# A weight ring's first refills in fewer transfers, on one core of Trainium2

## The chip, the core and the metric

One core of a Trainium2 chip runs the whole kernel. The metric is the device time of one execution in microseconds. The kernel before was run three times: 1255.82, 1257.26 and 1256.54 us, median 1256.54. Times inside a profile are counted from the first instruction of the profiled execution.

## The reference, cut to what matters

One layer of a streaming encoder on 256 tokens of width 1024, float32. A combined projection feeds two token mixers (RWKV-7 and a gated MLP over chunks), their gated sum goes through an output projection, and then comes the part that this case is about, a mixture of 32 experts, of which each token uses four:

```python
def expert_block(args):
    tok, e = args
    hgu = xt[tok] @ w_gate_up[e] + b_gate_up[e]
    gate = jnp.minimum(hgu[:, 0::2], SWIGLU_LIMIT)
    up = jnp.clip(hgu[:, 1::2], -SWIGLU_LIMIT, SWIGLU_LIMIT)
    act = gate * jax.nn.sigmoid(SWIGLU_ALPHA * gate) * (up + 1.0)
    return act @ w_down[e] + b_down[e]
```

`w_gate_up[e]` is 1024 x 2048 and `w_down[e]` 1024 x 1024, both float32: 12 MiB of weights for each expert, 384 MiB in all, and every byte of them is read once.

## The kernel before, in words

**Phases.** Up to about 340 us the kernel does the mixers and the output projection. Then it goes through the 32 experts in order (`moe`). Each expert has 64 slots for its tokens. TensorE gathers the tokens of a pair of experts by matmuls with a one-hot matrix, multiplies them with the expert's gate/up weights (`gate_up`, matmuls on L1602), transposes the activations, multiplies them with the down weights (`down`, L1627) and scatters the result back to the token rows in PSUM (`scatter`, L1656). Down and scatter of an expert run behind the gate/up of the next.

**Pieces and ring.** The weights are cut into 96 pieces (`PIECES`) of 4 MiB, 32 KB in each of 128 partitions: two for an expert's gate/up matrix and one for its down matrix. In each partition a piece is 32 KB in one run, in HBM and in SBUF. Their order is that in which TensorE reads them: 0 and 1 are gate/up of expert 0, 2 and 3 gate/up of expert 1, 4 down of expert 0, 5 and 6 gate/up of expert 2, 7 down of expert 1, 8 and 9 gate/up of expert 3, 10 down of expert 2, and so on. They go through a ring of five buffers (`RING`); piece n lies in buffer n mod 5. So piece 5 refills the buffer of piece 0, piece 7 that of piece 2, piece 12 that of piece 7.

**Who waits for whom.** TensorE counts `pieces_read` up by one for each quarter of a piece that it has multiplied with, four a piece (L1604, L1629). All loads of the ring are issued by SyncE, one after the other, on one queue (`weights`, from L461); before each it waits until TensorE has read that part of the piece that lay there. A load counts its buffer's semaphore `ring_full` up when it has landed. TensorE waits for that semaphore at the start of a piece for all loads of the piece (L1595, L1621), also where the piece came in several; only the last three pieces (`TAIL_PARTS`) have a semaphore for each part. How many loads a piece comes in is set by `fills(n)` (L348): four for piece 5, two for the other pieces below 10, one from piece 10 on. `fill_of` adds them up, so that both sides count alike, and in `weights` the part of the older piece that must have been read is worked out from it as well:

```python
for i in range(fills(n)):
    sp.wait_ge(sm["pieces_read"], quarters_read(*reader, 4 * (i + 1) // fills(n)))
    load_part(n, i, fills(n))
```

**The preload.** The first five pieces are loaded while the mixers still run, since their buffers lie where the mixers' data lay; a list written by hand (L440 to L459) gives the order of the halves and what each has to wait for: 0a, 0b, 2a, 1a, 1b, 3a, 2b, 4b, 3b, 4a (a and b are a piece's halves). The halves of piece 1 stand behind the wait for `y_done`, one behind the other, and that of piece 3 follows without a wait. The last two, 3b and 4a, wait for the output projection. `more_passes` would go through all experts again if one of them had more tokens than slots; with these inputs there is one pass, and the branch is not taken.

Of the kernel before, what the change touches and what calls it, by code (L numbers as in the profile page):

```python
# [67 lines left out]
def build(nc, cst, x, norm1_g, w_in, b_gate, time_mix, w_decay_up, w0, a_up, a0, g_up, k_k, k_a, r_k,  # L68
# [8 lines left out]
    with ctx:  # L77
# [95 lines left out]
        RING = len(SLOT_AT)  # L173
# [135 lines left out]
        unit_of = [("a", n, n % 8) for n in range(NA)] + [("v", n, 4 - 4 * n) for n in range(2)]  # L309
        unit_of += [("f", j, (2 * j + 4) % 8) for j in range(len(f_loads))] + [("o", k, (k + 4) % 8) for k in range(KT)]  # L310
        unit_load = {(kind, n): (u, 1 + sum(v == u for _, _, v in unit_of[:i])) for i, (kind, n, u) in enumerate(unit_of)}

        def unit_sem(kind, n):
# [31 lines left out]
        def slot_of(n):  # L345
            return n % RING

        def fills(n):  # L348

            return 4 if n == RING else 2 if n < 2 * RING else 1  # L350

        def fill_of(p, n):
            return p * sum(fills(m) for m in range(slot_of(n), PIECES, RING)) + sum(fills(m) for m in range(slot_of(n), n + 1, RING))
# [39 lines left out]
        def _(sp):  # L393
# [35 lines left out]
            def load(n, lo, hi, full):  # L429
                sp.dma_start(ring[slot_of(n)][:, lo:hi], pieces[n][:, lo:hi]).then_inc(full, 16)  # L430

            def load_part(n, i, parts=2):
                load(n, i * PIECE // parts, (i + 1) * PIECE // parts, ring_full[slot_of(n)])
# [13 lines left out]
            sp.wait_ge(sm["gl_done"], KT)  # L447
            load_part(2, 0)
            sp.wait_ge(sm["y_done"], NCH)
            load_part(1, 0)  # L450
            load_part(1, 1)
            load_part(3, 0)
            sp.wait_ge(sm["m_ready"], KT * NCH)
            load_part(2, 1)
# [6 lines left out]
            def weights(p, read_count=None):  # L461
                for n in range(RING if read_count is not None else 0, PIECES):
                    if read_count is not None and n == PIECES // 2:
                        read_count()
                    reader = (p, n - RING) if n >= RING else (p - 1, max(range(n, PIECES, RING)))
                    if n < 2 * RING:
# [3 lines that stand above are left out]
                    else:  # L470
                        sp.wait_ge(sm["pieces_read"], quarters_read(*reader))
                        if n in TAIL_PARTS:
                            load_tail(n)
                        else:
                            load(n, 0, PIECE, ring_full[slot_of(n)])
# [1275 lines left out]
```

## Time and profile before

| What | Before |
| --- | --- |
| Median of three runs | 1256.54 us |
| Profiled execution | 1257.94 us |
| Its span, first to last instruction | 1256.1 us |
| Granted TensorE clock, mean | 0.991 |
| TensorE busy | 1198.1 us, 95% of the span |
| VectorE, ScalarE busy | 293.6 us, 188.7 us |
| Moved by DMA | 447.78 MB, mean 356 GB/s |
| The queue with the ring's loads (q1) | 439.93 MB, 85.3% of 16 engines' time |
| Chain of waits that ended last | PE 71%, DMA 27% |

The span is what the profile shows; the execution's own time has 1.8 us around it. The granted clock is the share of TensorE's full clock that it was given. The chain of waits is followed back from the last instruction, at each step to what released it.

In the rows below, times are microseconds from the span's start. SPq is SyncE's queue: its rows are issues of transfers, and "DMA to landing" is the time from an issue to the last byte's arrival, as the semaphore tells it. All ring loads have the line L430. An issue itself takes 0.33 to 0.43 us. Landing time less issue time therefore holds the wait behind older transfers, too. Where two or three issues share a row, the times to landing are the least, the middle and the longest of them. In rows 3, 4 and for piece 9 a later issue has the longer time; for pieces 7 and 8 (two issues each, in the middle the mean) the first issue has the longer one and the second the shorter.

### The profile page before, as it was taken

How to read it: one execution, taken by the hardware profiler on the slowest of the kernel's cores; microseconds unless marked ns; L12 is line 12 of the kernel's file. 1: busy time of each engine (PE TensorE's matmuls, PEld its weight loads, DVE VectorE, ACT ScalarE, POOL GpSimd, SP SyncE). 2: the span in 40 equal slices, each digit the busy share in tenths (PEclk: the TensorE clock that was granted, in tenths of full speed). 3: DMA queues.
4: the chain of work that ended last, by engine and by line, in shares of the span. 5: the costliest groups of instructions: out<-in, count | busy, mean ns of one | idle time of the engine just before them, and what ended most of it. 6: DMA issues, size and time to landing. Idle time of an engine off the chain costs nothing.

```text
span 1256.1 us, 16267 instructions
## 1 busy us (share of the span) xinstructions
PE 1198.1 (95%) x7267; PEld 580.2 (46%) x7267; DVE 293.6 (23%) x639; ACT 188.7 (15%) x359; POOL 11.1 (1%) x24
## 2 busy tenths in 40 slices
PE   5999999999999999999998989999999989899997
PEld 4788668876533433434333333334333333333332
DVE  1155473334412111121111111111212111111111
ACT  2363212323200001000000100010000000000102
POOL 1000000000000000000000000000000000000000
PEclk9999999999999999999999999999999999999999
DMA  8451668347999999999999999999999999999994
GB/s 228 118 141 45 201 187 219 87 156 305 377 407 409 430 426 434 434 430 433 428 431 431 430 431 429 430 434 434 431 427 428 433 431 434 432 431 427 430 425 185
DMA packets 71244, 447.78 MB, mean 356 GB/s; under 512 B 12516, under 2 KB 51550, under 8 KB 56704
## 3 DMA queue, kind: packets, MB, share of 16 engines
q1 hardware_dynamic: 60864, 439.93, 85.3%
q0 software_dynamic: 1456, 4.36, 1.1%
q10 hardware_dynamic: 8848, 2.38, 0.8%
q8 instruction: 60, 0.98, 0.3%
q14 instruction: 16, 0.13, 0.0%
HBM read 444.56 MB, written 2.10 MB: 356 GB/s over the span
## 4 chain that ended last, share of the span: by engine, by line
PE 71%; DMA 27%; DVE 1%; issue 0%; ACT 0%; SPq 0%; DVEq 0%; ACTq 0%
PE ps L1602 27%; DMA ring<-w_gate_up 26%; PE ps L1213 8%; PE ps L1627 8%; PE ps L1301 7%; PE ps L1587 4%; PE ps L1656 3%; PE ps L1489 2%; PE ps L1288 2%; PE ps L1610 2%; PE ps L1646 1%; PE ps L1637 1%; PE ps L1241 1%; DMA consts<-cst 1%; PE ps L1551 1%; PE ps L1260 0%
## 5 line engine op out<-in xcount | busy, mean ns | idle before, releaser
L1602 PE MATMUL ps<-ring,xacc 128*64 128x512 f32 x2048 | 467.1, 603 | 27.0 <-DMA ring<-w_gate_up 25.6
L1602 PEld LDWEIGHTS ps<-ring,xacc 128*64 128x64 f32 x2048 | 144.0, 138 | 316.4 <-issue 310.1
L1627 PE MATMUL ps<-ring,aT 128*64 128x512 f32 x992 | 218.8, 593 | 7.5 <-DMA ring<-w_down 7.5
L1627 PEld LDWEIGHTS ps<-ring,aT 128*64 128x64 f32 x992 | 74.0, 137 | 148.1 <-issue 148.1
L1162 DVE TENSOR_SCALAR gc<-ps 128x512 f32<-128x512 f32 x32 | 22.1, 692 | 394.4 <-PE ps L1602 394.4
L1118 DVE TENSOR_TENSOR xacc<-ps,vec 128x512 f32<-128x512 f32 x32 | 22.1, 692 | 343.2 <-PE ps L1587 343.2
L1213 PE MATMUL ps<-hT,wbuf 128*128 128x256 f32 (+1 forms) x432 | 99.4, 388 | 2.8 <-DVE hT L811 2.8
L1213 PEld LDWEIGHTS ps<-hT,wbuf 128*128 128x128 f32 (+1 forms) x432 | 81.7, 191 | 18.4 <-issue 3.1
L1301 PE MATMUL ps<-hT,wbuf 128*128 128x256 f32 x384 | 85.9, 382 | 0.1
L1301 PEld LDWEIGHTS ps<-hT,wbuf 128*128 128x128 f32 x384 | 72.1, 190 | 11.8 <-issue 2.2
L770 ACT ACTIVATE sgm<-gc 128x512 f32<-128x512 f32 x32 | 20.2, 632 | 372.0 <-DVE gc L1162 372.0
L1587 PEld LDWEIGHTS ps<-oh,x2p 128*128 128x128 f32 x512 | 60.6, 194 | 27.6 <-issue 26.5
L1587 PE MATMUL ps<-oh,x2p 128*128 128x128 f32 x512 | 66.7, 284 | 0.9 <-DVE oh L1081 0.9
L1656 PE MATMUL ps<-ysl,oht 64*128 64x512 f32 x248 | 61.9, 616 | 0.7 <-ACT ysl L749 0.7
L759 ACT ACTIVATE oht<-ps 128x256 f32<-128x256 f32 x32 | 12.3, 384 | 253.7 <-PE ps L1637 253.7
L749 ACT ACTIVATE ysl<-ps 128x512 f32<-128x512 f32 x31 | 18.5, 597 | 177.3 <-PE ps L1627 177.3
L1610 PE MATMUL ps<-biases,consts 32*64 32x512 f32 x256 | 34.8, 612 | 0.0
L1169 DVE TENSOR_TENSOR gc<-uc,sgm 128x512 f32<-128x512 f32 x32 | 34.2, 1069 | 1.8 <-ACT sgm L770 0.8
L1656 PEld LDWEIGHTS ps<-ysl,oht 64*128 64x128 f32 x248 | 21.3, 186 | 21.5 <-issue 20.0
L1489 PE MATMUL ps<-wbuf,XM 128*128 128x512 f32 x64 | 28.5, 595 | 0.3 <-DVE XM L994 0.3
L1288 PE MATMUL ps<-wbuf,hT 128*128 128x512 f32 x64 | 28.0, 592 | 0.0
L1165 DVE SCALAR_TENSOR_TENSOR uc<-uc,gc 128x512 f32<-128x512 f32 x32 | 22.1, 692 | 1.1
(259 smaller groups left out, 677.4 us busy)
## 6 DMA issues: line engine op xcount, KB each, us to landing
ring<-w_gate_up SPq DMA_DIRECT2D x55, 4096.0 KB, 36.0
ring<-w_down SPq DMA_DIRECT2D x28, 4096.0 KB, 34.5
ring<-w_gate_up SPq DMA_DIRECT2D x16, 2048.0 KB, 11.6
wbuf<-w_in SPq DMA_DIRECT2D x26, 512.0 KB, 4.0
wbuf<-w_in SPq DMA_DIRECT2D x12, 1024.0 KB, 6.5
ring<-w_down SPq DMA_DIRECT2D x6, 2048.0 KB, 12.2
wbuf<-w_in SPq DMA_DIRECT2D x2, 2048.0 KB, 9.9
wbuf<-w_out SPq DMA_DIRECT2D x8, 512.0 KB, 4.8
```

Of the source, the lines that this page charges most:

```text
L1118: V.tensor_tensor(by_k(xT[pair % 2])[:, 4 * half:4 * half + 4, :], by_k(bank(b)), vec[:, r:r + 4].unsqueeze(2).to_broadcast([P, 4, 2 * SLO ...
L1162: V.tensor_scalar(gc[:, :], pairs[:, 0, :], LIMIT, None, ALU.min).then_inc(sm["gc_ready"], 1)
L1169: V.tensor_tensor(acts[:, :].rearrange("q (r p) -> q p r", r=4), by_row(uc), by_row(sgm), MUL).then_inc(sm["act_ready"], 1)
L1213: last = mm(proj_slot(n)[0:w, :], wv[:, k, 0:w], hv[:, k, :], start=k == 0, stop=k == KT - 1)
L1288: last = mm(bank(m_), hv[:, k, tb * P:(tb + 1) * P], wv[:, k, :], start=k == 0, stop=k == KT - 1)
L1301: last = mm(f_slot(t), wv[:, k, P * (t % 2):P * (t % 2) + P], hv[:, k, :], start=k == 0, stop=k == KT - 1, skip_group_check=True)
L1489: last = mm(bank(2 * tb + half_), XM_v[:, k, tb * P:(tb + 1) * P], unit((k + 4) % 8)[:, 512 * half_:512 * half_ + 512], start=k == 0, stop ...
L1587: last = mm(bank(b, (k % 4) * 2 * SLOTS, 2 * SLOTS), x2p[:, tb * D + k * P:tb * D + (k + 1) * P], oh[pair % 2][:, tb * 2 * SLOTS:(tb + 1) ...
L1602: last = mm(bank(GU_BANK + q, 0, 512, slice(64 * half, 64 * half + 64)), x_, w[:, :, half, :], start=k == 0, stop=k == KT - 1, skip_group_ ...
L1610: mm(bank(GU_BANK + q, 0, 512, slice(64 * half, 64 * half + 64)), ident[r, 32 * q + e:32 * q + e + 1].to_broadcast([32, SLOTS]), bgu[r, :] ...
L1627: last = mm(bank(b, 0, 512, slice(64 * half, 64 * half + 64)), turned[:, c0:c0 + SLOTS], w[:, D * r + 512 * half:D * r + 512 * (half + 1)] ...
L1656: last = mm(bank(OUT_BANK + 2 * tb + half), oht[e % 2][r, tb * P:(tb + 1) * P], slots[r, :], start=e == 0 and isinstance(p, int), stop=Fal ...
```

## The change

`fills` gives two loads to pieces 0, 2, 3, 4, 5 and 6 and one to all others. Piece 5 (`RING`) is thus refilled in halves and not in quarters, pieces 7, 8 and 9 in one load and not in halves, and piece 6 in halves as it was. In the preload the two halves of piece 1 become one load of the whole piece at the same place. The bytes, the buffers and TensorE's code stay as they are.

```diff
         def fills(n):
 
-            return 4 if n == RING else 2 if n < 2 * RING else 1
+            return 2 if n in (0, 2, 3, 4, RING, RING + 1) else 1
...
             sp.wait_ge(sm["y_done"], NCH)
-            load_part(1, 0)
-            load_part(1, 1)
+            load_part(1, 0, 1)
             load_part(3, 0)
             sp.wait_ge(sm["m_ready"], KT * NCH)
```

## Rows read from the trace of the kernel before

**Rows 1.** Engines' busy time by stretch (us, instructions), granted clock, DMA share, GB/s:

```profile
core 0: us, PE busy (x) PEld busy (x) DVE busy (x) ACT busy (x) POOL busy (x), PEclk, DMA share, GB/s
329.00:333.00 4.00, 3.60 (x17) 2.07 (x16) 1.96 (x6) 0.87 (x2) 0.00 (x0) 1.00 0.28 74
418.00:615.00 197.00, 197.00 (x990) 74.59 (x989) 32.74 (x65) 16.40 (x30) 0.00 (x0) 1.00 1.00 431
615.00:1200.00 585.00, 554.86 (x2702) 210.75 (x2698) 91.31 (x176) 44.59 (x81) 0.00 (x0) 0.99 1.00 431
```

**Rows 2.** TensorE's waits at the ring, 340 to 615 and 615 to 1240; one matmul group:

```profile
  DVE uc L1163: 1.4, 1
...
  DMA ring<-w_gate_up: 25.6, 14
...
1210.38 4.92 PE L1602 MATMUL ps<-ring,xacc 128*64 128x512 f32 x14 [2.64 <-DMA ring<-w_gate_up]
```

**Rows 3.** SyncE's issues from 303.3 to 304.5: 1a, 1b and 3a.

```profile
L430 SPq DMA_DIRECT2D ring<-w_gate_up x3: 327/432/434, 303.4 to 304.2; - x3
...
DMA to landing us min/median/max: 8.7/13.2/17.7
```

**Rows 4.** Issues of 3b and 4a, the preload's last, in this order of landing:

```profile
L430 SPq DMA_DIRECT2D ring<-w_gate_up x1: 328/328/328, 331.5 to 331.5; - x1
L430 SPq DMA_DIRECT2D ring<-w_down x1: 433/433/433, 331.9 to 331.9; - x1
...
DMA to landing us min/median/max: 7.4/10.8/14.2
```

**Rows 5.** Three issues: second quarter of piece 5, its fourth, second half of piece 6.

```profile
L430 SPq DMA_DIRECT2D ring<-w_gate_up x1: 327/327/327, 344.2 to 344.2; - x1
...
DMA to landing us min/median/max: 7.0/7.0/7.0
...
L430 SPq DMA_DIRECT2D ring<-w_gate_up x1: 327/327/327, 348.8 to 348.8; - x1
...
DMA to landing us min/median/max: 7.3/7.3/7.3
...
L430 SPq DMA_DIRECT2D ring<-w_gate_up x1: 328/328/328, 355.6 to 355.6; - x1
...
DMA to landing us min/median/max: 12.4/12.4/12.4
```

**Rows 6.** Issues of pieces 7, 8 and 9, two halves each, from 362.8:

```profile
L430 SPq DMA_DIRECT2D ring<-w_down x2: 328/328/328, 362.8 to 368.2; - x2
...
DMA to landing us min/median/max: 9.6/9.9/10.2
...
L430 SPq DMA_DIRECT2D ring<-w_gate_up x2: 327/328/328, 371.6 to 377.2; - x2
...
DMA to landing us min/median/max: 10.5/10.8/11.1
...
L430 SPq DMA_DIRECT2D ring<-w_gate_up x2: 328/328/328, 380.6 to 384.1; - x2
...
DMA to landing us min/median/max: 11.9/12.6/13.3
```

**Rows 7.** Issues of pieces 10, 11 and 12, one load each:

```profile
L430 SPq DMA_DIRECT2D ring<-w_down x1: 328/328/328, 395.5 to 395.5; - x1
...
DMA to landing us min/median/max: 12.1/12.1/12.1
...
L430 SPq DMA_DIRECT2D ring<-w_gate_up x1: 328/328/328, 402.4 to 402.4; - x1
...
DMA to landing us min/median/max: 16.4/16.4/16.4
...
L430 SPq DMA_DIRECT2D ring<-w_gate_up x1: 328/328/328, 409.3 to 409.3; - x1
...
DMA to landing us min/median/max: 19.2/19.2/19.2
```

## The prediction, before any result

> **What bounds the kernel now.** I read the stretches of the expert phase first: engines beside DMA share and rate. From 418 us to 1200 us the DMA share is 1.00 at 431 GB/s, in a stretch where TensorE never stops (418 to 615: busy 197.00 of 197.00 us) and in one where it does (615 to 1200: 554.86 of 585.00 us) [rows 1]. So the transfers run without a break from about 418 us on, and TensorE is at first ahead on a stock of loaded pieces and then runs out of it. The second view, what TensorE waited for at the ring, says the same: up to 615 us it waits for no weights at all, only 1.4 us for VectorE; after that 25.6 us for gate/up pieces in 14 waits, the last of which, 2.64 us long, ends at 1210.38 us, with only the last three pieces and the tail behind it [rows 2]. A stream that never pauses ends when it ends: **what counts is how far it has got at 418 us.** A microsecond that the 16 DMA engines lose before that comes out at the end, as long as that last wait is longer than zero; a microsecond that TensorE loses early does not.
>
> The third view is SyncE's issues one by one, each with its time to landing; issue plus time to landing gives when a piece is there. Two steady numbers come from it. Pieces 11 and 12 land at 402.4 + 16.4 = 418.8 and 409.3 + 19.2 = 428.5: **9.7 us for a whole piece** in an uninterrupted stream [rows 7]. The half of piece 3 issued at 331.5 lands 7.4 us later, at 338.9, and the half of piece 4 queued behind it at 331.9 + 14.2 = 346.1 [rows 4]; two halves of piece 8 land at 371.6 + 11.1 = 382.7 and 377.2 + 10.5 = 387.7 [rows 6]: **4.9 to 5.0 us for a half.** A half therefore costs the stream nothing more than half a whole, within 0.1 us.
>
> The third number is the price of an empty queue. The half issued at 331.5 found the engines idle (share 0.28 between 329 and 333 us [rows 1]) and took 7.4 us where 4.9 are data: **2.5 us to start** [rows 4]. Piece 10, a whole row issued at 395.5 when piece 9 had 1.9 us left to land (384.1 + 13.3 = 397.4), took 12.1 us [rows 6, 7]; less 9.7 of data that is 2.4. So a transfer issued with more than about 2.4 us of others still to land is free, and one issued with less loses the rest; piece 10 lost 0.5 us.
>
> **The change part by part.** Piece 1 in one transfer: today its halves and that of piece 3 are issued from 303.4 to 304.2 and land up to 304.2 + 17.7 = 321.9 [rows 3]. The same bytes go in the same order, with one issue of 0.4 us fewer. TensorE is done with piece 0 at 348.8, when the last quarter of piece 5 goes out [rows 5], so piece 1 has been there for some 27 us; and the queue runs dry anyhow from 329 to 333 us, where the engines are idle for 0.72 of 4 us, 2.9 us [rows 1]. That cover hides a gain as much as a loss; without it, the part would be worth the 0.1 us of a merged half. Cost 0. The wait in front of it stays, and nothing else on SyncE moves.
>
> Piece 5 in halves, not quarters: the first load now waits for half of piece 0 and not a quarter, so it goes at 344.2, the place of today's second quarter, and not before it. What is in front, the half of piece 4, lands at 346.1, which leaves 1.9 us, less than the 2.4 of a start. The first half lands at 344.2 + 7.4 = 351.6 (second quarter today: 344.2 + 7.0 = 351.2). The second is issued at 348.8 as today's fourth quarter and lands at 351.6 + 4.9 = 356.5 (today 348.8 + 7.3 = 356.1) [rows 5]. That is 0.4 us late, and so is piece 6, whose waits don't change: 368.4 for today's 355.6 + 12.4 = 368.0 [rows 5].
>
> Piece 7 whole: here the price is paid. Today its first half is issued at 362.8, as soon as half of piece 2 has been read, behind piece 6, and its second at 368.2; they land at 362.8 + 10.2 = 373.0 and 368.2 + 9.6 = 377.8 [rows 6]. Whole, it can only go when all of piece 2 has been read, at 368.2. By then piece 6 has landed or is within 0.2 us of it: the queue is empty, and piece 7 lands at 368.2 + 2.4 + 9.7 = **380.3, 2.5 us later than today.** The 0.4 us of piece 5 vanishes in this gap. Nothing but loads stands behind the waiting issue on SyncE, and their own waits end later.
>
> The start cost is the one term that I carry over rather than read. From below: if piece 10's excess were all due to what was in front of it, a start would cost nothing, and piece 7 would land at 377.9, no loss. From above the 2.5 us of the half into idle engines. I take 2.4, the row of a whole piece, and keep both ends. The Trainium skill (DMA: Bandwidth & Descriptors, Anatomy of one DMA) gives about 2.0 us as the fixed cost of a transfer beside its data; it speaks against this change, in that a queue let run dry pays this once, and with its figure the sum below would be 0.4 us smaller.
>
> Pieces 8 and 9 whole: piece 8 waits until 377.2, when piece 7 has 3.1 us to go, more than a start; it lands at 390.0. Piece 9 is issued at 384.1 and lands at 399.7, against 397.4: 2.3 late. Six fewer boundaries between transfers have given back 0.1 to 0.2. Piece 10 is issued at 395.5 as today, since TensorE's reading of piece 5 isn't touched. It now has 4.2 us in front of it, loses no start, and lands at 409.4, against 395.5 + 12.1 = 407.6: **1.8 us late.** TensorE needs piece 7 only after 402.4, the issue of piece 11, which waits for the end of reading piece 6 [rows 7]; so 20 us of stock cover the later landings, and no wait of TensorE is added before 615 us.
>
> **The sum:** +2.5 (a dry queue before piece 7) - 0.2 (whole rows) - 0.5 (piece 10's start now covered) = **+1.8 us**, carried by a full stream to the wait that ends at 1210.38. The profiled execution took 1257.94 us for a span of 1256.1, so its like would be 1259.7 and span 1257.9. It was 1.4 us above the median of the runs, 1256.54; the forecast for the median is 1256.54 + 1.8 = **1258.3 us**. A measurement of this kernel tells about 0.2% from no change, 2.5 us: the forecast is inside.
>
> **The rivals.**
> *One more long step (slower).* Piece 11 lands 418.8 - 407.6 = 11.2 us after piece 10, not 9.7, though its queue was full: a step 1.5 us too long, which the rows don't explain [rows 7]. There must be more of them: from 428.5 to the end of the last wait at 1210.4 there are 80 pieces, 781.9 us at 9.77 each [rows 2, 7], some 6 us over 80 x 9.7, so three or four more. That is one in about 210 us of unbroken stream. An idle queue forgives such a step, and today the last one is at 395 us; after the change it is at 368 us. The unbroken stretch is 27 us longer, and the chance that it holds a fifth step is 27 in 210, 13%. Then the time is 1256.5 + 1.8 + 1.5 = 1259.8, and slower. It decides where two pieces after piece 7 land 11.2 us apart and piece 11 still takes 11.2.
>
> *Hidden anyway (no change).* If the start cost is covered because the engines end piece 6 unevenly and take up piece 7 as each comes free, or if piece 10's lost 0.5 us and another step of today fall away, 0 to 0.3 us are left: 1256.6. For it: the bound from below above. Against: piece 10, which had even 1.9 us in front and took 12.1 us [rows 7].
>
> *Fewer transfers are worth their fixed cost (faster).* Six issues fewer: one for piece 1, two for piece 5, three for pieces 7 to 9. By the start cost of 2.4 us each, were it paid in line, 14 us would be saved: 1242. The third and fourth quarters of piece 5 take 4.9 us together (351.2 to 356.1), as one half does [rows 5], so the costs overlap wherever a queue stands. The same page of the Trainium skill (DMA: Bandwidth & Descriptors, Bandwidth) advises to batch transfers to 1 MiB or more; the quarters here are of 1 MiB, and these rows show nothing left to gain above it.
>
> *The change doesn't act:* the preload of piece 1 alone would be that case, 1256.5; but the waits of pieces 7 to 9 are written out in the loop and must move.
>
> **How the numbers follow.** Forecast 0.65, one more step 0.15, hidden or not acting 0.16, faster 0.04. The median of three runs moves by some 0.5 us, so of the forecast's share about one in six ends past 2.5 us. That gives slower 0.15 + 0.11 = 0.26, same 0.70, faster 0.04. The range goes from the hidden case less 0.5, 1256.0, to the case of one more step plus 0.6, 1260.4; it leaves out the faster case and the outer tails.
>
> **What would show it.** Right: the first load of piece 5 issued at 344.2, none at 362.8; piece 7 issued at 368.2 and landing near 380.3; the DMA share dips between 366 and 370 us and no longer near 395; piece 10 lands near 409.4; the last long wait on a gate/up piece ends near 1212.2. Wrong: piece 7 landing before 379; another wait of TensorE before 615 us; a landing of piece 10 at 407.6 or a last wait that ends where it does today; more than four steps of 11.2 us.

## The result, and the profile after

The change makes the kernel slightly slower: the median of 22 runs is 1258.45 us against 1257.17 us of 22 runs before, a ratio of 1.0013 with a 95% interval of 1.0007 to 1.0019, that is +1.6 us (0.9 to 2.4); the two medians by themselves lie 1.3 us apart, which is inside that interval. Forecast were +1.8 us and a median of 1258.3. The effect is real and inside the 0.2% that the prediction had called "same".

The profiled execution took 1258.22 us for a span of 1256.3, and the one before 1257.94 for 1256.1. These two differ by 0.3 us only, less than the runs do; the end of this section says why.

First the stretches, engines beside DMA share, of the kernel before (two that weren't shown above), then of the one after; columns as in [rows 1], the last two being DMA share and GB/s:

```profile
366.00:368.00 2.00, 2.00 (x12) 0.69 (x12) 0.00 (x0) 0.88 (x2) 0.00 (x0) 1.00 1.04 418
394.00:396.00 2.00, 2.00 (x12) 0.72 (x10) 0.00 (x0) 0.00 (x0) 0.00 (x0) 1.00 0.58 246
```

```profile
366.00:368.00 2.00, 2.00 (x12) 0.71 (x10) 0.00 (x0) 0.24 (x1) 0.00 (x0) 1.00 0.00 0
394.00:396.00 2.00, 2.00 (x12) 0.64 (x10) 0.00 (x0) 0.00 (x0) 0.00 (x0) 1.00 0.99 426
418.00:615.00 197.00, 196.67 (x986) 73.95 (x982) 32.99 (x66) 15.74 (x29) 0.00 (x0) 1.00 1.00 431
```

Before, the engines were idle for a moment near 395 us. Now they stand completely still from 366 to 368 us and are full near 395. From 418 us on both streams run at 431 GB/s without a break.

TensorE's waits at the ring after the change, 340 to 615 us, then 615 to 1240 us, and its last wait for a gate/up piece:

```profile
  DVE uc L1162: 1.4, 1
...
  DMA ring<-w_gate_up: 21.7, 13
  DMA ring<-w_down: 10.5, 8
...
1211.78 3.65 PE L1601 MATMUL ps<-ring,xacc 128*64 128x512 f32 x16 [2.63 <-DMA ring<-w_gate_up]
```

No wait ended before 615 us that wasn't there before, as in [rows 2]; the 0.33 us that TensorE stands still in the stretch up to 615 us are the start of its first wait for weights, which begins at 614.7. The last wait ends at 1211.78, not 1210.38.

SyncE's issues after the change: first and second half of piece 5, second half of piece 6, then pieces 7 to 12 in one load each.

```profile
L430 SPq DMA_DIRECT2D ring<-w_gate_up x1: 327/327/327, 343.5 to 343.5; - x1
...
DMA to landing us min/median/max: 7.2/7.2/7.2
...
L430 SPq DMA_DIRECT2D ring<-w_gate_up x1: 327/327/327, 348.1 to 348.1; - x1
...
DMA to landing us min/median/max: 8.0/8.0/8.0
...
L430 SPq DMA_DIRECT2D ring<-w_gate_up x1: 328/328/328, 354.9 to 354.9; - x1
...
DMA to landing us min/median/max: 11.8/11.8/11.8
...
L430 SPq DMA_DIRECT2D ring<-w_down x1: 328/328/328, 367.5 to 367.5; - x1
...
DMA to landing us min/median/max: 12.3/12.3/12.3
...
L430 SPq DMA_DIRECT2D ring<-w_gate_up x1: 328/328/328, 376.5 to 376.5; - x1
...
DMA to landing us min/median/max: 14.1/14.1/14.1
...
L430 SPq DMA_DIRECT2D ring<-w_gate_up x1: 328/328/328, 383.4 to 383.4; - x1
...
DMA to landing us min/median/max: 16.9/16.9/16.9
...
L430 SPq DMA_DIRECT2D ring<-w_down x1: 328/328/328, 394.9 to 394.9; - x1
...
DMA to landing us min/median/max: 15.1/15.1/15.1
...
L430 SPq DMA_DIRECT2D ring<-w_gate_up x1: 328/328/328, 401.7 to 401.7; - x1
...
DMA to landing us min/median/max: 18.1/18.1/18.1
...
L430 SPq DMA_DIRECT2D ring<-w_gate_up x1: 327/327/327, 408.6 to 408.6; - x1
...
DMA to landing us min/median/max: 20.9/20.9/20.9
```

Two profiled executions don't enter the expert phase at the same instant. The first issue behind the output projection [rows 4] came at 331.51 us before and at 330.82 after; I count from it in all that follows. Against that mark piece 7 lands at 379.8 + 0.7 = 380.5 (forecast 380.3), piece 12 at 429.5 + 0.7 = 430.2, 1.7 us later than in [rows 7], and the last wait ends (1211.78 - 330.82) - (1210.38 - 331.51) = **2.1 us later**.

That the spans differ by 0.2 us and not by more has two reasons: the expert phase began 0.7 us earlier, and the tail behind the last wait took 45.8 us before and 44.5 after. Here are 10.6 us behind the last wait, before (with the 3.4 us in them in which the clock was low) and after:

```profile
1210.40:1221.00 10.60, 10.60 (x46) 3.96 (x46) 0.00 (x0) 0.98 (x2) 0.00 (x0) 0.84 1.00 421
1210.60:1214.00 3.40, 3.40 (x10) 1.22 (x8) 0.00 (x0) 0.00 (x0) 0.00 (x0) 0.50 1.00 424
```

```profile
1211.80:1222.40 10.60, 10.60 (x54) 4.05 (x56) 0.00 (x0) 0.98 (x2) 0.00 (x0) 1.00 1.01 425
```

TensorE was granted 0.84 of its clock in the one, 1.00 in the other. Before, it had the lower of its two levels, 1.2 of 2.4 GHz, from 1210.6 to 1214.0 us. The first 24 matmuls behind the wait took 7.07 us or, in the experiments where that clock was full, 5.37. Behind the last wait TensorE is the path, and this costs an execution that meets it 1.7 us by the matmuls, 1.2 us by the two tails. Single profiled spans are therefore no measure of a change of this size; landings counted from the mark are, and many runs.

### The profile page after: what moved, and what is told of

Read it like the earlier page. It is cut to its first block, busy times and chain, and to the rows that moved or that the text cites. A ratio compares the mean times of both kernels' runs of the same rounds, so it can differ in the third digit from the quotient of the medians.

```text
span 1256.3 us, 16261 instructions
## 1 busy us (share of the span) xinstructions
PE 1199.5 (95%) x7267; PEld 580.3 (46%) x7267; DVE 293.4 (23%) x639; ACT 188.5 (15%) x359; POOL 11.0 (1%) x24
## 4 chain that ended last, share of the span: by engine, by line
PE 72%; DMA 26%; DVE 1%; issue 0%; ACT 0%; SPq 0%; DVEq 0%; ACTq 0%
PE ps L1601 27%; DMA ring<-w_gate_up 25%; PE ps L1212 8%; PE ps L1626 8%; PE ps L1300 7%; PE ps L1586 5%; PE ps L1655 3%; PE ps L1488 2%; PE ps L1287 2%; PE ps L1609 2%; PE ps L1645 1%; PE ps L1636 1%; PE ps L1240 1%; PE ps L1550 1%; DMA consts<-cst 1%; PE ps L1259 0%
## 5 line engine op out<-in xcount | busy, mean ns | idle before, releaser
L758 ACT ACTIVATE oht<-ps 128x256 f32<-128x256 f32 x32 | 12.3, 383 | 249.4 <-PE ps L1636 249.4
```

## The experiments

Nine kernels. Theory A is that of the prediction: a transfer pays 2.4 us of start as far as the queue in front of it doesn't cover that, and each such loss before the stream closes reaches the end. The table gives for each the ratio to runs of the kernel before on the same chip, and how much later in us piece 12 landed and the last wait ended, from one profile each and counted from the mark:

| Kernel | Ratio (95%) | Piece 12 | End of last wait |
| --- | --- | --- | --- |
| the change | 1.0013 (1.0007 to 1.0019) | +1.7 | +2.1 |
| only piece 7 whole | 1.0009 (1.0000 to 1.0018) | +1.9 | +1.9 |
| the change, 7 in halves | 0.9998 (0.9989 to 1.0007) | +1.1 | +1.1 |
| 5 to 9 whole | 1.0027 (1.0017 to 1.0037) | +2.1 | +2.9 |
| 1 whole, 5 in halves | 1.0000 (0.9991 to 1.0010) | -0.1 | -0.1 |
| before, 10 to 14 in halves | 0.9991 (0.9981 to 1.0000) | -1.0 | -0.9 |
| before, finer preload | 1.0002 (0.9993 to 1.0011) | -0.4 | -0.1 |
| the last two together | 0.9985 (0.9976 to 0.9994) | -1.5 | -1.5 |
| 4096 empty instructions | 1.0075 (1.0062 to 1.0089) | +6.7 | +10.7 |
| 1024 of them, later | 1.0003 (0.9994 to 1.0012) | +0.3 | +0.2 |

**Only piece 7 whole.** The kernel before with one entry of `fills` changed.

```diff
-            return 4 if n == RING else 2 if n < 2 * RING else 1
+            return 4 if n == RING else 1 if n == RING + 2 else 2 if n < 2 * RING else 1
```

> Piece 7 in one load, everything else as before (piece 5 in quarters, 8 and 9 in halves, piece 1 in two). Theory A (one dry queue): the whole loss of the change sits in front of piece 7. It is issued at about 368 us into an empty queue and lands 12.1 us later, 2.5 us later than its second half did; piece 10 then has more than 2.4 us in front and loses no start. Time: before +1.8 us, the same as the full change. Theory B (every refill that has to wait for more of an older piece adds its share): one of four such refills, +0.5 us. Theory C (whole rows cost or gain nothing, the difference is scatter between runs): +0.0 us and piece 10 landing where it did.

Piece 7 landed at the same place as in the full change (380.3 by the mark, for 380.5) and the last wait ended 1.9 us late; the runs say +1.1 us (0 to 2.3). By the trace piece 7 alone carries the loss. Theory C, that nothing moves, is out by the landings; the runs alone hardly tell it from A, since their interval begins at 0. B's +0.5 lies within that interval too, and it is the +1.9 us of the trace that speaks against it.

**The change with piece 7 in halves.**

```diff
-            return 2 if n in (0, 2, 3, 4, RING, RING + 1) else 1
+            return 2 if n in (0, 2, 3, 4, RING, RING + 1, RING + 2) else 1
```

> The full change, but piece 7 stays in halves. Theory A: the dry queue moves one piece on. Piece 7's second half lands near 378.2, piece 8 is issued whole at 377.2 with 1.0 us in front of it, too little to cover a start of 2.4, and lands at 389.3 instead of 387.7; pieces 9 and 10 follow 9.7 us apart, and piece 10 loses no start. Time: before +1.1 us, between before and the full change. If undoing piece 7 alone brought back the whole loss (+0.0), theory A would be wrong about piece 8. Theory B: three of four shares, +1.3 us, and no visible gap in front of piece 8.

The issue of piece 8:

```profile
L430 SPq DMA_DIRECT2D ring<-w_gate_up x1: 328/328/328, 376.4 to 376.4; - x1
...
DMA to landing us min/median/max: 13.4/13.4/13.4
```

Issued at 376.4 with 0.4 us of piece 7 in front of it, piece 8 took 13.4 us: its data, the start of 2.4, and another 1.3 that fit the long steps (the experiments on code, further down). The start is paid one piece further on, and the last wait ends the forecast 1.1 us late. The runs give -0.3 us (-1.4 to +0.9), which leaves +1.1 just outside; taken alone they would say that A is wrong about piece 8. Eleven runs hardly carry a tenth of a per cent: the trace bears A out, the runs don't, and the result stays half settled.

**Pieces 5 to 9 whole.**

```diff
-            return 2 if n in (0, 2, 3, 4, RING, RING + 1) else 1
+            return 2 if n in (0, 2, 3, 4) else 1
```

> Pieces 5 to 9 all in one load each, piece 1 too. Piece 5 then goes only when all of piece 0 has been read (348.8 us) and lands near 360.9, 4.8 us later than before; piece 6 near 371 to 372. Theory A (only the last dry queue before the stream closes counts): piece 7 can't be issued before 368.2 in any case, so the stream behind it is where the full change has it, and the 4.8 us are swallowed: before +1.8 us (up to 2.2), the same as the full change. Theory B (losses add up): +1.8 and +4.8 or at least +4 us.

Issue of piece 7, and TensorE's last wait:

```profile
L430 SPq DMA_DIRECT2D ring<-w_down x1: 328/328/328, 366.1 to 366.1; - x1
...
DMA to landing us min/median/max: 13.3/13.3/13.3
...
1211.23 7.07 PE L1601 MATMUL ps<-ring,xacc 128*64 128x512 f32 x24 [2.64 <-DMA ring<-w_gate_up]
```

+3.4 us in the runs (2.1 to 4.6), +2.9 at the last wait. By the mark, piece 5 landed 4.8 us late and piece 6 3.8 us, so adding up (B: +1.8 and at least +4 on top, +5.8) is refuted: most of that is swallowed by the wait for TensorE in front of piece 7. But A's +1.8, up to 2.2, was too low by about one microsecond. Piece 6 was still in flight when piece 7 was issued: there was no idle queue any more to hide piece 6's long step (5 landed at 358.8, 6 at 369.8, 11.0 us apart), and piece 7 followed 9.7 us behind, at 379.45. By the mark it lands at 381.5, 1.0 us later than in the full change. The missing term was the long steps.

**Piece 1 whole and piece 5 in halves.**

```diff
-            return 4 if n == RING else 2 if n < 2 * RING else 1
+            return (1 if n == 1 else 2) if n < 2 * RING else 1
...
-            load_part(1, 0)
-            load_part(1, 1)
+            load_part(1, 0, 1)
```

> Only the first part of the change: piece 1 in one load and piece 5 in halves; pieces 6 to 9 in halves as before. Theory A: piece 5 and all behind it land 0.3 to 0.4 us later up to piece 9, and piece 10, which lost 0.5 us of a start before, makes that good: before +0.0 us, piece 10's landing unchanged. Theory B: +0.4 us. A gain (under -0.5 us) would say that fewer transfers are worth something of their own.

1.0000 (-1.1 to +1.3 us in the runs), and -0.1 us at the last wait. These two parts of the change cost nothing and bring nothing; that even B's +0.4 is too much is told by the trace alone.

**Halves up to piece 14.** If a start is lost in front of piece 10, one can win it back.

```diff
-            return 4 if n == RING else 2 if n < 2 * RING else 1
+            return 4 if n == RING else 2 if n < 3 * RING else 1
...
-                    if n < 2 * RING:
+                    if n < 3 * RING:
```

> The kernel before, with pieces 10 to 14 in halves as well. Theory A (a start is lost only where less than 2.4 us of transfers are in front): piece 10's first half goes when half of piece 5 has been read, about 388 us, so the 0.5 us that piece 10 loses today is not lost: the time is before -0.5 us. Theory D on the long steps (each load of instructions, one per expert or about every 26 us, occupies one of the 16 engines, eight in turn; the first after an idle queue sets the whole stream back by its length, 1.4 us, and the next seven hide behind it): with no idle queue at 395 us the stream is unbroken from 333 us, the long step at piece 11 vanishes and the later ones move from 615, 840 and 1055 us to about 570, 790, 1000 and 1200; piece 12 lands 1.9 us earlier than before, at about 426.6, and the last wait only 0.5 us earlier. Theory E (long steps come at fixed times): piece 12 lands 0.5 us earlier and the steps stay where they are.

-1.1 us in the runs (-2.4 to 0), -0.9 at the last wait; A's -0.5 is in the interval. On the long steps: the one at piece 11 vanished, and the later ones came with the landings at 593, 818 and 1023 us instead of 615, 840 and 1055. So they don't sit at fixed times, against E. They moved together, by 22, 22 and 32 us: by one load of instructions and not by two, as D had it, since the first fell on piece 9. Piece 12 was therefore 1.0 us early and not 1.9, and the last wait 0.9 and not 0.5.

**Finer preload, to fill the idle stretch at 329 us.**

```diff
-            return 4 if n == RING else 2 if n < 2 * RING else 1
+            return 4 if n in (3, RING) else 2 if n < 2 * RING else 1
...
-            load_part(3, 0)
+            load_part(3, 0, 4)
+            load_part(3, 1, 4)
...
             load_part(4, 1)
+            load_part(3, 3, 4)
             sp.wait_ge(sm["out_done"], 2 * TB)
-            load_part(3, 1)
+            load_part(3, 2, 4)
```

> The kernel before, with piece 3 in quarters throughout; its last quarter, whose place is free before the output projection ends, is issued right behind the second half of piece 4, so that it fills the idle stretch from 329 to 333 us; the rest as before. Theory A: the preload's last half then lands near 341.8 instead of 346.1, but the quarters of piece 5 can't be issued earlier (342.4 and on) and pay a start, so piece 5 lands 1.4 us earlier and pieces 6 to 9 with it; piece 10, issued at 395.5, then finds 0.5 us in front of it, pays the whole start, and lands at 407.6 as before: +0.0 us in all. If a microsecond of idle engines in the preload were worth a microsecond at the end, it would be -1.4 us or more.

Second half of piece 9, and piece 10:

```profile
L430 SPq DMA_DIRECT2D ring<-w_gate_up x1: 328/328/328, 382.8 to 382.8; - x1
...
DMA to landing us min/median/max: 13.4/13.4/13.4
...
L430 SPq DMA_DIRECT2D ring<-w_down x1: 328/328/328, 394.3 to 394.3; - x1
...
DMA to landing us min/median/max: 12.0/12.0/12.0
```

Nothing came of it in all, as forecast: 1.0002. But the way there was another. The mark is at 330.26 in this trace, so 1.25 us are to be added. The preload's last half landed at 341.7 + 1.25 = 343.0, 3.1 us earlier than before and not 4.3; piece 5, whose quarters still wait for TensorE, was 0.4 us early (355.7 for 356.1) and not 1.4; and piece 9 landed at 396.2 + 1.25 = 397.4, where it did before, since some steps in front were longer than 4.9. Piece 10 was thus issued with the same 1.9 us in front as before, and not with 0.5, took 12.0 us, a start and its data, and landed 0.1 us earlier. Idle engines in the preload weren't worth their time at the end, but that piece 10 takes such a gain back isn't shown here, as none had reached it.

**Both together.** The two edits above in one kernel.

> The finer preload and halves up to piece 14 together. Theory A: no start is lost after 343 us, so the 1.4 us of the one and the 0.5 us of the other both reach the end: before -1.9 us, piece 12 landing near 425 (with the long step moved as in the kernel with halves alone). If the two don't add, the first refills' own waits for TensorE hold the stream, and it is -0.5 us as with halves alone.

```profile
1206.81 7.07 PE L1604 MATMUL ps<-ring,xacc 128*64 128x512 f32 x24 [2.63 <-DMA ring<-w_gate_up]
```

-1.9 us in the runs (-3.0 to -0.8), as forecast, and -1.5 at the last wait; piece 12 landed at 427.1 by the mark, not near 425. By its ratio this kernel is faster than both that of before and the changed one. That the preload's gain comes on top of the halves' is less sure: the traces say 0.6 us (-1.5 for -0.9), not the 1.4 of A, and the intervals of the two kernels' runs overlap widely.

**More code.** 4096 empty instructions on GpSimd behind its last transfer. They compute nothing, and nobody waits for them.

```diff
             pool.dma_start(nf[:, :], norm_f_g.partition_broadcast(P)).then_inc(sm["nf_in"], 16)
+            for i in range(4096):
+                pool.engine_nop()
```

> The kernel before, with 4096 empty instructions on GpSimd behind its last transfer (from about 340 us), where it is idle otherwise; nothing waits for them. Theory D (loads of instructions make the long steps): their code is 256 KB, 16 more loads of 16 KB on the instruction queue, two more rounds over eight engines: two more long steps of 1.4 us, before +2.8 us, and instruction packets rise from 60 to about 76. Theory E (something else makes the long steps): +0.0 us, with the packets there all the same.

The DMA queues (packets, MB, share of 16 engines) from 345 to 515 us, before and with the added code, and the issues of pieces 12 and 13 of the latter:

```profile
q8 instruction: 7, 0.11, 0.3%
q14 instruction: 3, 0.02, 0.0%
```

```profile
q14 instruction: 33, 0.27, 0.4%
q8 instruction: 6, 0.10, 0.2%
...
L430 SPq DMA_DIRECT2D ring<-w_gate_up x1: 328/328/328, 409.2 to 409.2; - x1
...
DMA to landing us min/median/max: 26.0/26.0/26.0
...
L430 SPq DMA_DIRECT2D ring<-w_down x1: 328/328/328, 422.0 to 422.0; - x1
...
DMA to landing us min/median/max: 24.2/24.2/24.2
```

Thirty more packets of 8 KB, 0.25 MB beside 71 MB, and pieces land some 11 us apart (435.2 to 446.2 here) in place of 9.7. In all +9.5 us in the runs and +10.7 at the last wait: loads of instructions do set the stream back, and far more than their bytes at 431 GB/s would, 0.6 us. On one engine alone, which has a sixteenth of that rate, they would take 9.7 us (an estimate: 32 x 8 KB at 27 GB/s), most of what was lost. D was right in kind and wrong in form: the loads were of 8 KB on another queue, q14, 32 of them at 10.7 / 32 = 0.3 us each, or 0.5 if the 5.9 us of ordinary long steps that they hid are counted in, and not 16 of 16 KB at 1.4 us in two rounds. One thing told more than the sum: behind 515 us the ordinary long steps were gone, none above 0.1 us up to the end.

**Less code, later.** That called for a test of whether such delays add or hide behind each other.

```diff
             pool.dma_start(nf[:, :], norm_f_g.partition_broadcast(P)).then_inc(sm["nf_in"], 16)
+            pool.wait_ge(sm["ysl_out"], 8)
+            for i in range(1024):
+                pool.engine_nop()
```

> The kernel before, with 1024 empty instructions on GpSimd, held back until eight experts are done (about 560 us), in the middle of the unbroken stream. Their code is 64 KB, 8 loads of 8 KB. In the kernel with 4096 of them 32 such loads put one engine 10.7 + 5.9 us behind, 0.5 us each, and the ordinary long steps (5.9 us in all) vanished behind it. Theory D (a piece lands when the slowest of 16 engines is done, and delays on different engines hide behind each other): the stream is set back by 4.2 - 1.4 = 2.8 us between 560 and 605 us, then the ordinary long steps at 615 and 840 vanish behind that, and the one near 1055 us comes through; since the ordinary ones add up to 5.8 us, more than 4.2, the last wait ends where it did: before +0.0 us. If delays add whatever engine they fall on: 8 x 0.33 = +2.7 us up to +4.2 us at the end, with the ordinary steps all in their places.

First the issues of two pieces in the kernel before, at 801 and 808 us, the second with the longer time. Then, with the added code, the instruction queue from 540 to 640 us, the issues of two pieces there, and of two at 803 and 810 us:

```profile
L430 SPq DMA_DIRECT2D ring<-w_gate_up x2: 327/328/328, 801.4 to 808.2; - x2
...
DMA to landing us min/median/max: 27.0/29.1/31.3
```

```profile
q14 instruction: 8, 0.07, 0.2%
...
L430 SPq DMA_DIRECT2D ring<-w_gate_up x1: 328/328/328, 568.0 to 568.0; - x1
...
DMA to landing us min/median/max: 36.5/36.5/36.5
...
L430 SPq DMA_DIRECT2D ring<-w_down x1: 328/328/328, 580.9 to 580.9; - x1
...
DMA to landing us min/median/max: 34.6/34.6/34.6
...
L430 SPq DMA_DIRECT2D ring<-w_gate_up x1: 328/328/328, 803.3 to 803.3; - x1
...
DMA to landing us min/median/max: 25.8/25.8/25.8
...
L430 SPq DMA_DIRECT2D ring<-w_gate_up x1: 328/328/328, 810.4 to 810.4; - x1
...
DMA to landing us min/median/max: 28.5/28.5/28.5
```

The pieces that land at 593, 604 and 615 us do so after 10.2, 11.0 and 11.0 us (the last: 604.5 to 615.5), 3.1 us over; the kernel before is 1.5 us over there, in one step at 615. So at 615 us the stream is set back by 1.6 us more than there, a little over the expected 4.2 less two ordinary steps, 1.4. The ordinary step of 11.2 us near 840 us, there in the kernel before (pieces at 828.4 and 839.5), has vanished (829.1 to 838.9, 9.8 us), and that near 1055 us has come through. The last wait ends 0.2 us late, and the runs say +0.4 us (-0.8 to +1.5): the sum of 2.7 us or more is refuted. **Such delays don't add up: the smaller ones hide behind the largest.**

That they fall on different engines can be seen in the traces' single packets. Each ring load ends with 16 packets of 4 bytes, taken here as one of each engine, and lands 0.3 to 0.5 us behind the last of them. In the kernel before, the 16 of piece 10 lie within 0.5 us. At piece 11, behind a load of instructions at 413.1, one comes 1.2 us behind the other 15. With each of the next seven such loads one more falls back to it, until eight stand there at 593.7 us and eight still 0.8 us or more ahead; the next load, at 610.2, sets one of them back again, and that is the step at 615. So the ordinary loads, those on q8, meet eight engines in turn, and in this kernel only the first of each round costs. With the 4096 added instructions a single one falls behind the other 15, by 5.7, 7.0 and 8.5 us at pieces 11, 12 and 13: all of their loads meet one engine. **A piece lands when the most delayed engine is done.**

## Why the prediction was right

**The bound.** A full stream from 418 us on, and a last wait longer than zero, so that any loss before comes out at the end: right. The stream runs at 431 GB/s behind 418 us as it did, and what piece 12 has lost or won, the last wait shows again within 0.4 us, but for two kernels: that with pieces 5 to 9 whole (2.1, then 2.9) and that with more code, whose added loads went on behind piece 12.

**The start of a transfer into an empty queue, 2.4 us,** the one term carried over: piece 7 took 12.3 us, which less 9.7 is 2.6, and the engines stood at a share of 0.00 from 366 to 368 us. In two more kernels a whole piece was issued into an empty queue, piece 7 where it alone was whole and piece 5 where 5 to 9 were: both took 12.1 us, a start of 2.4. The bound from below, no cost at all, is out. The Trainium skill (DMA: Bandwidth & Descriptors, Anatomy of one DMA) fits 2.0 us to transfers that GpSimd issues; these are issued by SyncE, and the measured figure is the larger.

**Piece 5 in halves, 0.4 us and swallowed; piece 1, nothing:** 356.1 + 0.7 = 356.8 for the forecast 356.5, and the kernel with these parts alone stands at 1.0000.

**Piece 7, +2.5:** +2.7 by the mark (380.5 for 377.8). The kernel with piece 7 alone changed holds the whole loss.

**Pieces 8 to 10:** here single landings were wrong. Piece 8 came 10.8 us behind piece 7 and not 9.7, so that piece 10 landed at 410.0 + 0.7 = 410.7, not 409.4. Against the kernel before, pieces 7 to 11 were 2.7, 3.6, 3.6, 3.1 and 1.7 us late. Piece 11 came 9.8 us behind piece 10 and not 11.2: a long step had changed places, from piece 11 to piece 8, and from there on the forecast was met again, with 420.5 for 418.8 + 1.8. The prediction left piece 11's long step where it was; that one step was traded for one of nearly the same size is luck, and without the trade the last wait would have ended about a microsecond later. The term "-0.5, piece 10's start now covered" is borne out: piece 10 came 9.7 us behind piece 9, and 10.2 before. The halves up to piece 14 point the same way (-0.9 at the last wait), though their runs, -2.4 to 0, hardly tell it from nothing. The -0.2 for whole rows is too small to be read apart from the long step in piece 8.

**The sum,** +1.8: +1.6 by the runs, +2.1 by the last wait.

**The rivals.** The long steps were given one chance in seven to turn the result, as if they fell by lot, one in 210 us of stream. They don't: there are four large ones before, 11.1 to 11.2 us at 419, 615, 840 and 1055 us, and four after, 10.6 to 10.8 us at 391, 596, 821 and 1026. After the change four small ones stand between them, 10.1 to 10.3 us at 517, 733, 938 and 1163; with them the last wait ends 0.4 us later than piece 12 would have it. That the number of large ones stayed is what saved the forecast, and nothing in it said so; in the kernel with pieces 5 to 9 whole their sum grew, and A missed by a microsecond. "Hidden anyway" and "fewer transfers are worth their fixed cost" are out, the first with an interval that begins at +0.9 us, the second with the 1.0000 of the kernel with three transfers fewer.

What stays open: which of the 16 engines these are, and why a load of instructions costs more than its own packet's time. The 32 added ones took 0.31 us each in the trace and, where the stream was whole (six pieces, 435.1 to 501.4 us, with 12 such loads), set it back by 0.66 us each. Open too is why the change with piece 7 in halves measured -0.3 us where its own trace shows +1.1.

## What to carry to other kernels

In a stream of loads that is the bound, a coarser transfer costs nothing while others stand in front of it, and costs up to a whole start, 2.4 to 2.6 us here, where its longer wait for a free place lets the queue run dry. Count for each load what is still in flight at its issue, and split those where it is less than the start. What is lost ahead of such a place is swallowed at it for the most part, as the kernel with pieces 5 to 9 whole shows. A gain should be taken back there in the same way, and so far that is seen only in small: with piece 1 whole and 5 in halves, piece 9 landed 0.4 us early by the mark and piece 10 0.1 us late. If so, such places are best mended from the last to the first. For effects of this size compare landings from a common mark, not spans.

## What the runs showed of the hardware that was not expected

Loads of instructions go through the same DMA engines as data and weigh far more than their bytes: 0.25 MB beside 71 MB lengthened the kernel by 9.5 us, 4096 empty instructions on an engine nobody waits for. A piece spread over 16 engines lands with the last of them, so that a delay on one engine counts fully, and smaller delays on others count nothing: 1024 empty instructions in the middle of the stream moved the last wait by 0.2 us.

TensorE's granted clock fell to 0.50 for 3.4 us right behind the last wait in some executions and stayed at 1.00 in others, with the same work and the same wait of 2.6 us ahead of it; 24 matmuls took 7.07 or 5.37 us. That is as large as the whole effect of this change.
